# A streaming encoder step: row blocks of the up-projection loaded by GpSimd, and the row projection's operands placed alike within 512 bytes

## Chip, cores and metric

The kernel runs on one core of a Trainium2 chip, as one launch. The metric is the device time of that launch in microseconds (us). The comparison is between medians of runs; the profile is of one execution.

## What is computed

One inference step of an encoder trunk of depth 1, for 2048 prompt rows and 64 sample rows with the same weights, all float32. Cut to what the change touches:

```python
x = layer_norm(x, ln_in_g, ln_in_b)                       # 2112 rows x 1024
q, k, v, z, xbc, dt_raw, u, vc = split_cols(x @ w_in, IN_SIZES)
...                                                       # attention, SSD scan, gated MLP, RMS norms
x = layer_norm(DN_ALPHA * x + mixed @ w_out, ln1_g, ln1_b)
up, ffn_conv_state = causal_dwconv(x @ ffn_w_in, ffn_conv_prev, ffn_conv_w, ffn_conv_b)
gate, val = split_cols(up, (D_FF, D_FF))                  # D_FF = 2816
x = layer_norm(DN_ALPHA * x + (jax.nn.silu(gate) * val) @ ffn_w_out, ln2_g, ln2_b)
```

## The kernel before

Seven stages follow one another: row projection, feature projection, attention, SSD and gated MLP, output projection, up-projection (`ffn_up`), down-projection. Every float32 product is three matmuls on rounded parts: high x high, high x low, low x high (`products`, lines 129 to 131; lines 3037 to 3039 in the up-projection). For that each operand is split: a cast to the high part on ScalarE, a subtraction for the low part on VectorE.

**Row projection** (`project_rows`, tensor names `pr_`). The columns of `w_in` that are wanted by rows (v, z, the two gated-MLP parts and dt: 1286) are loaded in eight k blocks of 128 rows into `w_raw`, and split into `w_hi` and `w_lo`, both [128, 8, 1286]. Seventeen row tiles of 128 rows follow. A tile is normalised, turned by eight transposes into `ps_t` (line 449), copied and split into `xt_hi` and `xt_lo`, and is then the stationary operand of 72 matmuls into `ps_y`: 24 each against columns 0 to 511, 512 to 1023 and 1024 to 1285. In tile 0 k is the outer loop, since the weights are still arriving; in the others the column group is.

Where these operands start in a partition, by the built program, modulo 512 bytes:

| operand | before | after |
|---|---|---|
| `w_hi`, 512-wide columns | 256 + 24 k | 256 |
| `w_lo`, 512-wide columns | 448 + 24 k | 256 |
| high part, last 262 columns | 256 + 24 k | 256 + 24 k |
| low part, last 262 columns | 448 + 24 k | 448 + 24 k |
| `xt_hi`, `xt_lo` (each k block 512 bytes long) | 128 | 256 |

In the output projection, which runs the same 128x128 by 512 matmuls (`mo_ps_y`), weights and rows all start at 384.

**Up-projection** (`ffn_up`, names `fu_`). The rows are taken in three passes (q = 0, 1, 2) of 704 rows, each as two halves of 352, and the product of a 2 x 2 block matrix is formed with seven products in place of eight (Winograd's form). A unit is one step j of 22 in a pass: it takes 128 columns of the gate half and 128 of the value half of `ffn_w_in`, and has 7 products x 4 k blocks x 3 = 84 matmuls of 354 (in the last pass 356) columns. `mm_done` counts products, seven a unit.

The pass's rows lie in `xb`, seven slots of [4 k blocks x 356]. Four of them are loaded from `x1t`, the turned rows of the stage before (`X_B11`, `X_B21`, `X_T1`, `X_B22`, 708 KB each), and the others are differences that VectorE makes in units 20 and 21 of the pass before (`differences`). Once all seven slots are split into `x_hi` and `x_lo` (`x_lo_done` at 7 for each pass), `xb` may be loaded again. Pass 0's blocks are loaded in the output projection. Those of pass q + 1 are loaded by `load_x` on SyncE at the end of unit 1 of pass q. Its order there is written out by hand in `body`: per unit the raw weights for unit j + 2 (`load_raw`, line 2452), the stores of the previous unit's results (`store_h`: `h_mix` from `val1`, line 2501, `h_val` from `val0`, line 2506; `store_sums`), the store of the split weights to `fu_w_split` in pass 0 and their load in passes 1 and 2 (lines 2553 and 2559), and in pass 1 loads and stores of `load_late` and `store_late`. SyncE issues all of these in that order, each after its wait.

ScalarE writes `val0` again for the next unit (`tap0_c21`) once `h_stored[0]` says that the last store of it has landed, and `val1` likewise with `h_stored[1]`. Behind that instruction on ScalarE stands the copy of TensorE's first product of the unit (`p1`, line 2728), without which TensorE's third product does not start.

In `ffn_up` GpSimd does only two small memsets (lines 2655 and 2656), once `x_lo_done` is at 14.

Of the kernel before, what the change touches and what calls it, by code (L numbers as in the profile page):

```python
# [26 lines left out]
P = 128  # L27
# [124 lines left out]
def project_rows(nc, d):  # L152
# [8 lines left out]
    with nc.cleanup_on_exit(), ExitStack() as ctx:  # L161
# [15 lines left out]
        w_hi, w_lo = m.sb("w_hi", [P, KD, NW], F32R), m.sb("w_lo", [P, KD, NW], F32R)  # L177
        x = m.sb("x", [P, 2, D])
        xr = m.sb("xr", [P, 2, D])
        xt_hi, xt_lo = m.sb("xt_hi", [P, 2, KD, P], F32R), m.sb("xt_lo", [P, 2, KD, P], F32R)  # L180
# [45 lines left out]
        with nc.Block() as block:  # L226
# [87 lines left out]
            def _(act):  # L314
                def weights_hi(ks):
                    for k in ks:
                        act.wait_ge(w_loaded[k], 64)
                        act.copy(w_hi[:, k, :], w_raw[:, k, :]).then_inc(w_hi_done, 1)
# [48 lines left out]
            def _(dve):  # L367
                def weights_lo(ks):
                    for k in ks:
                        dve.wait_ge(w_hi_done, k + 1)  # L370
                        dve.tensor_tensor(w_lo[:, k, :], w_raw[:, k, :], w_hi[:, k, :].bitcast(F32),
                                          ALU.subtract).then_inc(w_lo_done, 1)
# [68 lines left out]
            def _(pe):  # L441
# [12 lines left out]
                def step(t, p, i):  # L454
# [10 lines left out]
                    def product(k, x):  # L465
                        out, a, w = x
                        return products(pe, out, xt_hi[:, p, k, :n], xt_lo[:, p, k, :n],
                                        w_hi[:, k, a:a + w], w_lo[:, k, a:a + w], k == 0, k == KD - 1)
# [1802 lines left out]
def ffn_up(nc, d):  # L2271
# [12 lines left out]
    with nc.cleanup_on_exit(), ExitStack() as ctx:  # L2284
# [71 lines left out]
            "xb_zeroed", "rest_loaded", "xb_loaded", "t_done", "x_hi_done", "x_lo_done", "s_done", "w_hi_done", "w_lo_done"))  # L2356
        raw_loaded = [m.sem("raw_loaded0"), m.sem("raw_loaded1")]
# [86 lines left out]
        with nc.Block() as block:  # L2444
            @block.sync
            def _(sp):
# [10 lines left out]

                def x_block(slot, ks, g, q, done):
                    r = PW * q + 352 * g
                    if q == NQ - 1:  # L2460
                        sp.dma_start(xb[:, slot, :, 0:GAP], d["x1t"][:, ks, r - H:r + LASTP]).then_inc(done, 16)
                        if g:
                            sp.dma_start(xb[:, slot, :, SMP:], d["x1t"][:, ks, SEQ:ROWS]).then_inc(done, 16)
                        else:
                            sp.dma_start(xb[:, slot, :, GAP:], d["x1t"][:, ks, r + LASTP - H:r + 352]).then_inc(done, 16)
                    elif r == 0:
                        sp.dma_start(xb[:, slot, :, H:H + 352], d["x1t"][:, ks, 0:352]).then_inc(done, 16)
                    else:
                        sp.dma_start(xb[:, slot, :, 0:H + width(q)], d["x1t"][:, ks, r - H:r + width(q)]).then_inc(done, 16)

                def load_x(q):
                    lo_k, hi_k = slice(0, KH), slice(KH, KD)
                    x_block(X_B11, lo_k, 0, q, xb_loaded[0])
                    x_block(X_B21, hi_k, 0, q, xb_loaded[1])
                    x_block(X_T1, lo_k, 1, q, rest_loaded)
                    x_block(X_B22, hi_k, 1, q, rest_loaded)
# [88 lines left out]
                def body(q, j, p):  # L2565
# [37 lines left out]
                    if isinstance(j, int) and j == 1 and q + 1 < NQ:  # L2603
                        sp.wait_ge(x_lo_done, 7 * (q + 1))
                        load_x(q + 1)
# [10 lines left out]
            def loaded_x(q):  # L2616

                return (16 * (q + 1), 32 * (q + 1)) if q < NQ - 1 else (16 * q + 32, 32 * q + 64)

            def differences(eng, q):  # L2620
# [5 lines left out]
                def t3_step():  # L2626
                    eng.wait_ge(xb_loaded[0], loaded_x(q)[0])
                    eng.wait_ge(xb_loaded[1], loaded_x(q)[0])
                    eng.wait_ge(rest_loaded, loaded_x(q)[1])
                    eng.wait_ge(xb_zeroed, 2 if q == NQ - 1 else 1)  # L2630
                    if q == NQ - 1:
                        eng.wait_ge(late_stored, 16 * LATE)
                    if q:
                        eng.wait_ge(x_lo_done, 7 * q)
                    eng.tensor_tensor(t3, b22, b12, ALU.subtract).then_inc(t_done, 1)
# [16 lines left out]
            @block.gpsimd  # L2652
            def _(pool):
                pool.wait_ge(x_lo_done, 7 * (NQ - 1))
                pool.memset(xb[:, X_T1, :, GAP:SMP], 0.0)
                pool.memset(xb[:, X_B22, :, GAP:SMP], 0.0).then_inc(xb_zeroed, 1)

            @block.scalar
            def _(act):
# [16 lines left out]
                def split_x_hi(q, slot):  # L2676
                    n = H + width(q)
                    if slot < 2:
                        act.wait_ge(xb_loaded[slot], loaded_x(q)[0])
                        act.wait_ge(xb_zeroed, 1)  # L2680
                    else:
                        act.wait_ge(t_done, 4 * q + {X_T2: 3, X_T1: 2, X_T3: 1, X_B22: 1, X_T4: 4}[slot])
                    if q:
                        act.wait_ge(mm_done, 7 * (KF * q - 1) + slot + 1)
                    act.copy(x_hi[:, slot, :, :n], xb[:, slot, :, :n]).then_inc(x_hi_done, 1)
# [880 lines left out]
```

## Time and profile before

| | us |
|---|---|
| median of three runs | 2599.79 |
| lowest and highest of them | 2592.39, 2600.45 |
| profiled execution | 2602.54 |
| its span, first to last instruction | 2601.0 |

| part of the span | from, us | to, us |
|---|---|---|
| row projection, TensorE | 12.8 | 281.9 |
| output projection, 48 matmuls of one tile | 1000.79 | 1011.78 |
| up-projection, pass 0, units 0 to 21 | 1185.5 | 1516.6 |
| pass 1 | 1516.6 | 1836.0 |
| pass 2 | 1836.0 | 2143.9 |

The engines are PE (TensorE; PEld is its loading of the stationary operand), DVE (VectorE), ACT (ScalarE), POOL (GpSimd) and SP (SyncE); SPq and POOLq are their instruction queues, which issue DMAs. A row of the timeline is the start, the duration, the instruction, and in brackets how long its engine had been idle before it and who ended that. A duration on TensorE overlaps the next, so matmuls are compared by their starts. Idle time costs something only on an engine that is waited for. [...]

### The profile page before, as it was taken

Reading aid. Unit: us, or ns where it says so; the run is one execution under the profiler, and the core shown is the slowest. Engines: PE = TensorE matmul, PEld = TensorE weight load, DVE = VectorE, ACT = ScalarE, POOL = GpSimd, SP = SyncE. Lnnn points to the kernel's source line nnn. Section 1 sums busy time; section 2 is a strip of 40 time slices with the busy share of each in tenths; the row PEclk is TensorE's granted clock in tenths of the full one; section 3 lists DMA queues with packets and bytes.
Section 4 is the critical chain, followed back from the end, with each engine's and each line's share of the span. In section 5 each row is a group of like instructions: output and inputs, shape, how many; then the busy total and the mean of one; then the engine's idle time right before and its main releaser. Section 6 shows DMA issues by size and latency. Waiting matters only on the chain. (4 is left out here: it accounts for less than half of the span.)

```text
span 2601.0 us, 45346 instructions
## 1 busy us (share of the span) xinstructions
PE 2489.1 (96%) x14723; PEld 2301.3 (88%) x14723; DVE 1798.1 (69%) x3398; ACT 1117.2 (43%) x2109; POOL 199.4 (8%) x271
## 2 busy tenths in 40 slices
PE   6999999998999989998999999999999999999998
PEld 5888899998999978887999989999899998888787
DVE  5434375556776777787899987777877775455787
ACT  4445322225665542325555554444545453322231
POOL 0001100020002850110000000000000000000000
PEclk9999999998998989999999999999999999999999
DMA  6446565556544654647777789998787867575564
GB/s 209 146 143 213 178 212 189 194 176 161 134 126 136 196 173 157 210 155 247 256 243 248 233 281 335 300 309 281 262 262 251 263 201 209 141 221 144 163 172 140
DMA packets 466762, 537.65 MB, mean 207 GB/s; under 512 B 68170, under 2 KB 388204, under 8 KB 465218
## 3 DMA queue, kind: packets, MB, share of 16 engines
q1 hardware_dynamic: 442204, 452.25, 55.9%
q0 software_dynamic: 19408, 62.38, 7.4%
q10 hardware_dynamic: 5030, 21.46, 2.4%
q8 instruction: 71, 1.16, 0.2%
q14 instruction: 49, 0.40, 0.0%
HBM read 349.87 MB, written 189.00 MB: 207 GB/s over the span
## 5 line engine op out<-in xcount | busy, mean ns | idle before, releaser
L3037 PE MATMUL fu_banks<-mo_fu_x_hi,mo_fu_w 128*128 128x354 f32 (+1 forms) x1848 | 608.4, 329 | 37.7 <-DVE fu_c L2994 12.8
L3039 PE MATMUL fu_banks<-mo_fu_x_hi,mo_fu_w 128*128 128x354 f32 (+1 forms) x1848 | 603.8, 327 | 0.0
L3038 PE MATMUL fu_banks<-fu_x_lo_rest,mo_fu_w 128*128 128x354 f32 (+1 forms) x1584 | 517.5, 327 | 0.0
L3037 PEld LDWEIGHTS fu_banks<-mo_fu_x_hi,mo_fu_w 128*128 128x128 f32 x1848 | 351.4, 190 | 51.6 <-DVE mo_fu_w L2850 11.7
L3039 PEld LDWEIGHTS fu_banks<-mo_fu_x_hi,mo_fu_w 128*128 128x128 f32 x1848 | 351.7, 190 | 0.0
L3038 PEld LDWEIGHTS fu_banks<-fu_x_lo_rest,mo_fu_w 128*128 128x128 f32 x1584 | 301.4, 190 | 0.0
L3302 ACT CAST fu_fd_h_hi<-fu_fd_h_raw 128x768 fp32r<-128x768 f32 (+1 forms) x116 | 88.1, 760 | 255.4 <-DMA fu_fd_h_raw<-fd_h_sum 104.3
L3347 DVE TENSOR_TENSOR fu_fd_h_a<-fu_fd_h_raw,fu_fd_h_hi 128x768 fp32r<-128x768 f32 x108 | 95.6, 889 | 147.1 <-ACT fu_fd_h_hi L3302 147.0
L129 PE MATMUL pr_ps_y<-pr_w_hi,pr_xt_hi 128*128 128x512 f32 (+3 forms) x408 | 148.3, 364 | 5.0 <-DVE pr_xt_lo L406 5.0
L130 PE MATMUL pr_ps_y<-pr_w_lo,pr_xt_hi 128*128 128x512 f32 (+3 forms) x408 | 147.5, 362 | 0.0
L131 PE MATMUL pr_ps_y<-pr_w_hi,pr_xt_lo 128*128 128x512 f32 (+3 forms) x408 | 146.8, 360 | 0.0
L2691 ACT ACTIVATE fu_gate<-fu_c,fu_vecs 128x352 f32<-128x352 f32 (+1 forms) x132 | 90.1, 682 | 74.8 <-DVE fu_c L2974 67.9
L2868 DVE SCALAR_TENSOR_TENSOR fu_gate<-fu_c,fu_vecs,fu_gate 128x352 f32<-128x352 f32 (+1 forms) x132 | 76.9, 583 | 58.9 <-ACT fu_gate L2691 58.9
L1432 PE MATMUL at_ps_o<-pf_at_v,at_pt 128*128 (+2 forms) x900 | 111.7, 269 | 0.0
L129 PE MATMUL mo_ps_y<-sg_mo_w_hi,sg_mo_mt_hi 128*128 128x512 f32 (+1 forms) x272 | 108.2, 398 | 2.7 <-PEq L1481 2.7
L1432 PEld LDWEIGHTS at_ps_o<-pf_at_v,at_pt 128*128 128x128 f32 (+1 forms) x900 | 107.9, 191 | 1.1
L130 PE MATMUL mo_ps_y<-sg_mo_w_lo,sg_mo_mt_hi 128*128 128x512 f32 (+1 forms) x272 | 106.6, 392 | 0.0
L131 PE MATMUL mo_ps_y<-sg_mo_w_hi,sg_mo_mt_lo 128*128 128x512 f32 (+1 forms) x272 | 106.6, 392 | 0.0
L129 PE MATMUL fu_banks<-fu_fd_wa,fu_fd_h_hi 128*128 128x512 f32 x256 | 100.2, 392 | 4.3 <-DVE fu_fd_h_a L3347 3.4
L2845 DVE TENSOR_TENSOR mo_fu_w<-fu_w_raw,mo_fu_w 128x1024 fp32r<-128x1024 f32 x65 | 79.5, 1223 | 29.4 <-ACT mo_fu_w L2664 29.4
L130 PE MATMUL fu_banks<-fu_fd_wa,fu_fd_h_hi 128*128 128x512 f32 x256 | 99.7, 389 | 0.0
L131 PE MATMUL fu_banks<-fu_fd_wa,fu_fd_h_a 128*128 128x512 f32 x256 | 99.6, 389 | 0.0
(458 smaller groups left out, 5987.0 us busy)
## 6 DMA issues: line engine op xcount, KB each, us to landing
mo_fu_w<-fu_w_split SPq DMA_DIRECT2D x176, 512.0 KB, 5.0
fu_w_split<-mo_fu_w SPq DMA_DIRECT2D x44, 1024.0 KB, 5.8
fu_w_raw<-ffn_w_in SPq DMA_DIRECT2D x87, 512.0 KB, 5.4
fd_w_sum<-pf_fdw_sum ACTq DMA_DIRECT2D x11, 1024.0 KB, 5.0
fu_w_raw<-ffn_w_in SPq DMA_DIRECT2D x44, 256.0 KB, 6.0
pf_fdw_raw<-ffn_w_out ACTq DMA_DIRECT2D x9, 1024.0 KB, 8.0
x_rows<-pr_xr SPq DMA_DIRECT2D x16, 512.0 KB, 2.9
xt<-pr_xt SPq DMA_DIRECT2D x16, 512.0 KB, 4.0
```

The source lines that it names most:

```text
L129: pe.matmul(out, lhs_hi, rhs_hi, start=first, stop=False)
L130: pe.matmul(out, lhs_hi, rhs_lo, start=False, stop=False)
L131: return pe.matmul(out, lhs_lo, rhs_hi, start=False, stop=last)
L1432: last = pe.matmul(ps_o[:b.nq, par, 0:HD], pt[:w, par, k, :b.nq], vals, start=(k == 0), stop=(k == b.nb - 1))
L2691: act.activation(out, src[:, 0:n], ACT.Identity, bias=one(vecs[:, 3, :], mt), scale=one(vecs[:, 0, :], mt)).then_inc(tap0_done, 1)
L2845: dve.tensor_tensor(w_lo[:, p, W_A11:W_A12 + 1], w_raw[:, p, 0].rearrange("p (a k) c -> p a k c", a=2), w_hi[:, p, W_A11:W_A12 + 1].bitcas ...
L2868: dve.scalar_tensor_tensor(out=out, in0=src[:, 1:1 + n], scalar=one(vecs[:, 1, :], mt), in1=out, op0=ALU.mult, op1=ALU.add).then_inc(tap1_ ...
L3037: pe.matmul(out, wh, xh, start=first and k == 0, stop=False, skip_group_check=True)
L3038: pe.matmul(out, wh, xl, start=False, stop=False, skip_group_check=True)
L3039: last = pe.matmul(out, wl, xh, start=False, stop=k == KH - 1, skip_group_check=True)
L3302: act.copy(h_hi[:, n % RING, 0:raw.shape[1], 0:raw.shape[2]], raw).then_inc(h_hi_done, 1)
L3347: dve.tensor_tensor(low, raw, high.bitcast(F32), ALU.subtract).then_inc(h_lo_done, 1)
```

## The change

The first part splits the row projection's weights: the first 1024 columns keep the names `w_hi` and `w_lo`, now [128, 8, 1024], and the last 262 get tensors of their own, `w_hi_b` and `w_lo_b`. A tensor of 128 bytes that nobody uses, `beside`, stands before `xt_hi`. The table above has the places that come of it. Each of the eight casts and eight subtractions of the weights is now two instructions. The feature projection's operands keep their places.

The second part takes `load_x` from SyncE. GpSimd issues the same DMAs: for pass q, after `x_lo_done` at 7 q, the four blocks one at a time, block n after `mm_done` at 7 (22 (q - 1) + 3 n + 5), that is when unit 3 n + 4 of the pass before is done: at the starts of units 5, 8, 11 and 14. One semaphore, `x_loaded`, counts them, and both ScalarE and VectorE wait for all of a pass's. For pass 2 GpSimd does its memsets first.

```diff
-        w_hi, w_lo = m.sb("w_hi", [P, KD, NW], F32R), m.sb("w_lo", [P, KD, NW], F32R)
+
+        NA = 1024
+        w_hi, w_lo = m.sb("w_hi", [P, KD, NA], F32R), m.sb("w_lo", [P, KD, NA], F32R)
+        w_hi_b, w_lo_b = m.sb("w_hi_b", [P, KD, NW - NA], F32R), m.sb("w_lo_b", [P, KD, NW - NA], F32R)
         x = m.sb("x", [P, 2, D])
         xr = m.sb("xr", [P, 2, D])
+        beside = m.sb("beside", [P, 32])
...
-                        act.copy(w_hi[:, k, :], w_raw[:, k, :]).then_inc(w_hi_done, 1)
+                        act.copy(w_hi[:, k, :], w_raw[:, k, 0:NA])
+                        act.copy(w_hi_b[:, k, :], w_raw[:, k, NA:]).then_inc(w_hi_done, 1)
...
-                        dve.tensor_tensor(w_lo[:, k, :], w_raw[:, k, :], w_hi[:, k, :].bitcast(F32),
+                        dve.tensor_tensor(w_lo[:, k, :], w_raw[:, k, 0:NA], w_hi[:, k, :].bitcast(F32), ALU.subtract)
+                        dve.tensor_tensor(w_lo_b[:, k, :], w_raw[:, k, NA:], w_hi_b[:, k, :].bitcast(F32),
                                           ALU.subtract).then_inc(w_lo_done, 1)
...
-                        return products(pe, out, xt_hi[:, p, k, :n], xt_lo[:, p, k, :n],
-                                        w_hi[:, k, a:a + w], w_lo[:, k, a:a + w], k == 0, k == KD - 1)
+                        high, low = (w_hi[:, k, a:a + w], w_lo[:, k, a:a + w]) if a < NA else (w_hi_b[:, k], w_lo_b[:, k])
+                        return products(pe, out, xt_hi[:, p, k, :n], xt_lo[:, p, k, :n], high, low, k == 0, k == KD - 1)
...
-                    if isinstance(j, int) and j == 1 and q + 1 < NQ:
-                        sp.wait_ge(x_lo_done, 7 * (q + 1))
-                        load_x(q + 1)
...
             def _(pool):
-                pool.wait_ge(x_lo_done, 7 * (NQ - 1))
-                pool.memset(xb[:, X_T1, :, GAP:SMP], 0.0)
-                pool.memset(xb[:, X_B22, :, GAP:SMP], 0.0).then_inc(xb_zeroed, 1)
+                def x_block(slot, ks, g, q):
+                    r = PW * q + 352 * g
+                    if q == NQ - 1:
+                        pool.dma_start(xb[:, slot, :, 0:GAP], d["x1t"][:, ks, r - H:r + LASTP]).then_inc(x_loaded, 16)
+                        if g:
+                            pool.dma_start(xb[:, slot, :, SMP:], d["x1t"][:, ks, SEQ:ROWS]).then_inc(x_loaded, 16)
+                        else:
+                            pool.dma_start(xb[:, slot, :, GAP:], d["x1t"][:, ks, r + LASTP - H:r + 352]).then_inc(x_loaded, 16)
+                    else:
+                        pool.dma_start(xb[:, slot, :, 0:H + width(q)], d["x1t"][:, ks, r - H:r + width(q)]).then_inc(x_loaded, 16)
+
+                lo_k, hi_k = slice(0, KH), slice(KH, KD)
+                for q in range(1, NQ):
+
+                    pool.wait_ge(x_lo_done, 7 * q)
+                    if q == NQ - 1:
+                        pool.memset(xb[:, X_T1, :, GAP:SMP], 0.0)
+                        pool.memset(xb[:, X_B22, :, GAP:SMP], 0.0).then_inc(xb_zeroed, 1)
+                    for n, (slot, ks, g) in enumerate(((X_B11, lo_k, 0), (X_B21, hi_k, 0), (X_T1, lo_k, 1), (X_B22, hi_k, 1))):
+
+                        pool.wait_ge(mm_done, 7 * (KF * (q - 1) + 3 * n + 5))
+                        x_block(slot, ks, g, q)
```

SyncE in pass 0, from unit 0's last issues over unit 1 to the loop that begins with unit 2, before (`mo_fu_xb` is `xb`, `fu_val` is `val0` or `val1`):

```order
L2452 DMA fu_w_raw<-ffn_w_in 128x8x128 x2
L2501 DMA fd_h_mix<-fu_val 128x352
L2506 DMA fd_h_val<-fu_val 128x352
L2553 DMA fu_w_split<-mo_fu_w 128x2x1024 x2
L2469 DMA mo_fu_xb<-x1t 128x4x354 x4
L2387 UNCONDITIONAL_BRANCH
```

and after:

```order
L2459 DMA fu_w_raw<-ffn_w_in 128x8x128 x2
L2488 DMA fd_h_mix<-fu_val 128x352
L2493 DMA fd_h_val<-fu_val 128x352
L2540 DMA fu_w_split<-mo_fu_w 128x2x1024 x2
L2394 UNCONDITIONAL_BRANCH
```

The four loads are gone from the end of unit 1, and the raw weights for unit 4 (the loop's first DMA) follow the weight stores. At the same place of pass 1 eight loads are gone in the same way.

GpSimd in the up-projection, before:

```order
L2652 UNCONDITIONAL_BRANCH
L2655 MEMSET mo_fu_xb 128x4x2
L2656 MEMSET mo_fu_xb 128x4x2
L2444 UNCONDITIONAL_BRANCH
```

and after:

```order
L2640 UNCONDITIONAL_BRANCH
L2651 DMA mo_fu_xb<-x1t 128x4x354 x4
L2658 MEMSET mo_fu_xb 128x4x2
L2659 MEMSET mo_fu_xb 128x4x2
L2645 DMA mo_fu_xb<-x1t 128x4x290
L2649 DMA mo_fu_xb<-x1t 128x4x66
```

Twelve DMAs now stand on GpSimd's queue, four with 354 columns in pass 0, and in pass 1 eight: four of 290 columns, two of 66 and two of 64.

## Rows read from the trace of the kernel before

**Rows 1.** The page's busy time, share of the span and instructions of each engine.

```profile
PE 2489.1 (96%) x14723; PEld 2301.3 (88%) x14723; DVE 1798.1 (69%) x3398; ACT 1117.2 (43%) x2109; POOL 199.4 (8%) x271
```

**Rows 2.** Waits of TensorE, whole span: engine, tile, line, releaser: us in total, times, longest.

```profile
PE fu_banks L3037 <- DVE fu_c L2994: 12.8, 26, 1.6
PE fu_banks L3037 <- ACT fu_part L2728: 9.0, 4, 3.7
```

**Rows 3.** Timeline of TensorE: start, us, line, operands; row projection, then output projection.

```profile
163.73 0.48 PE L129 MATMUL pr_ps_y<-pr_w_hi,pr_xt_hi 128*128 128x512 f32 x1
...
174.96 0.28 PE L129 MATMUL pr_ps_y<-pr_w_hi,pr_xt_hi 128*128 128x262 f32 x1
...
1000.79 0.48 PE L129 MATMUL mo_ps_y<-sg_mo_w_hi,sg_mo_mt_hi 128*128 128x512 f32 x1
...
1011.78 0.49 PE L2237 MATMUL mo_ps_t<-ident,mo_y 128*128 128x128 f32 x3
```

**Rows 4.** Waits of ScalarE in the up-projection's passes 0 and 1 (1206 to 1836 us).

```profile
ACT fu_val L2691 <- DMA fd_h_val<-fu_val: 7.1, 1, 7.1
ACT fu_val L2691 <- DMA fd_h_mix<-fu_val: 5.9, 1, 5.9
```

**Rows 5.** SyncE queue timeline: end of unit 1, passes 0 and 1; last row unit 6.

```profile
1220.67 5.34 SPq L2469 DMA_DIRECT2D mo_fu_xb<-x1t  x4
...
1231.83 2.92 SPq L2501 DMA_DIRECT2D fd_h_mix<-fu_val  x1
...
1549.21 1.31 SPq L2461 DMA_DIRECT2D mo_fu_xb<-x1t  x1
...
1557.26 1.32 SPq L2463 DMA_DIRECT2D mo_fu_xb<-x1t  x1
...
1564.60 0.43 SPq L2506 DMA_DIRECT2D fd_h_val<-fu_val  x1
...
1616.02 0.37 SPq L2506 DMA_DIRECT2D fd_h_val<-fu_val  x1
```

**Rows 6.** Units 3, 9 (pass 0), 3, 9, 8 (pass 1): us, busy, clock, DMA, GB/s.

```profile
1235.49:1254.77 19.28, 15.98 (x87) 15.12 (x85) 13.79 (x22) 9.61 (x16) 0.00 (x0) 0.91 0.76 260
1326.27:1340.42 14.15, 13.92 (x85) 13.64 (x85) 13.21 (x21) 8.17 (x14) 0.00 (x0) 1.00 0.77 248
1562.88:1581.99 19.11, 15.45 (x86) 15.16 (x85) 10.87 (x21) 6.10 (x11) 0.00 (x0) 0.91 1.08 363
1650.80:1664.73 13.93, 13.93 (x86) 13.64 (x85) 10.54 (x21) 6.30 (x11) 0.00 (x0) 1.00 0.89 282
1637.15:1650.80 13.65, 13.65 (x86) 13.65 (x85) 10.21 (x20) 6.41 (x11) 0.00 (x0) 1.00 1.06 341
```

**Rows 7.** Groups of ScalarE's casts by width, and TensorE's first product of the row projection.

```profile
L318 ACT CAST pr_w_hi<-pr_w_raw 128x1286 fp32r<-128x1286 f32 x8 | 9.9, 1263 | 6.7 <-DMA pr_w_raw<-w_in 6.6
...
L2664 ACT CAST mo_fu_w<-fu_w_raw 128x1024 fp32r<-128x1024 f32 x20 | 20.7, 1036 | 0.0
...
19.77 0.80 PE L129 MATMUL pr_ps_y<-pr_w_hi,pr_xt_hi 128*128 128x512 f32 x1 [4.99 <-DVE pr_xt_lo L406]
```

**Rows 8.** Windows: pass 1 from unit 6 to 19, and 3 us of pass 0.

```profile
1609.50:1802.00 192.50, 192.50 (x1175) 190.50 (x1174) 144.90 (x266) 88.40 (x155) 0.00 (x0) 1.00 0.97 308
1321.00:1324.00 3.00, 2.74 (x17) 2.45 (x15) 2.65 (x4) 2.77 (x5) 0.00 (x0) 1.00 0.13 46
```

**Rows 9.** Stores of fu_val (pass 1), and timeline of ScalarE in unit 3 and unit 7.

```profile
DMA to landing us min/median/max: 1.9/4.6/5.3
...
1569.57 0.64 ACT L2691 ACTIVATE fu_val<-fu_banks,fu_vecs 128x352 f32<-128x352 f32 x1 [7.07 <-DMA fd_h_val<-fu_val]
...
1623.52 0.65 ACT L2691 ACTIVATE fu_val<-fu_banks,fu_vecs 128x352 f32<-128x352 f32 x1 [0.71 <-PE fu_banks L3039]
```

**Rows 10.** Timeline of VectorE and of GpSimd's queue in the row projection.

```profile
173.75 1.28 DVE L400 SCALAR_TENSOR_TENSOR pr_xr<-pr_xr,pr_rs,pr_b_bc 128x1024 f32<-128x1024 f32 x1
...
174.42 0.53 POOL L267 DMA_DIRECT2D pr_x<-x_prompt  x1 [15.70 <-DVE pr_xr L397]
```

More of the change, by code:

```diff
@@ L2356, in ffn_up @@
             "xb_zeroed", "rest_loaded", "xb_loaded", "t_done", "x_hi_done", "x_lo_done", "s_done", "w_hi_done", "w_lo_done"))
+        x_loaded = m.sem("x_loaded")
         raw_loaded = [m.sem("raw_loaded0"), m.sem("raw_loaded1")]
@@ L2456, in load_raw @@
                         load_half(j, p, half, raw_loaded[p], q)
[L2458 to L2476, printed above, removed]
                 load_half(0, 0, 1, raw_loaded[0])
@@ L2614, in _, with x_there @@
                     sp.wait_ge(w_stored[p], 32 * (KF // 2))
-            def loaded_x(q):
-                return (16 * (q + 1), 32 * (q + 1)) if q < NQ - 1 else (16 * q + 32, 32 * q + 64)
+            def x_there(eng, q, slot=None):
+                if q:
+                    eng.wait_ge(x_loaded, 16 * (4 if q < NQ - 1 else 12))
+                    return
+                for s in range(2) if slot is None else (slot,):
+                    eng.wait_ge(xb_loaded[s], 16)
+                if slot is None:
+                    eng.wait_ge(rest_loaded, 32)
             def differences(eng, q):
@@ L2626, in t3_step @@
                 def t3_step():
-                    eng.wait_ge(xb_loaded[0], loaded_x(q)[0])
-                    eng.wait_ge(xb_loaded[1], loaded_x(q)[0])
-                    eng.wait_ge(rest_loaded, loaded_x(q)[1])
+                    x_there(eng, q)
                     eng.wait_ge(xb_zeroed, 2 if q == NQ - 1 else 1)
@@ L2678, in split_x_hi @@
                     if slot < 2:
-                        act.wait_ge(xb_loaded[slot], loaded_x(q)[0])
+                        x_there(act, q, slot)
                         act.wait_ge(xb_zeroed, 1)
```

## The prediction

> **What bounds the kernel now.** First the busy shares: TensorE is busy 96% of the span [rows 1], so only two things can shorten the kernel: less time per matmul, or fewer of the gaps in which TensorE has nothing to do. TensorE's waits in the up-projection are mostly for VectorE's `fu_c`, 12.8 us in 26, and for ScalarE's `fu_part`, 9.0 us in only 4 [rows 2]: many small ones and a few large. Second, the timeline of TensorE: the row projection and the output projection run the same matmul, 128x128 against 512 columns. Durations overlap, so I go by starts. In the row projection the 48 matmuls of 512 columns of one row tile go from 163.73 to 174.96 us, 11.23 us, 234 ns each; in the output projection 48 go from 1000.79 to 1011.78, 10.99 us, 229 ns each [rows 3]. [...] Third, the waits of ScalarE in the up-projection: over the first two passes it waits for a transfer twice only, once 7.1 us (for the store of `fu_val` to `fd_h_val`) and once 5.9 us (the store to `fd_h_mix`) [rows 4]. Fourth, SyncE's queue at these two places: the four loads of `mo_fu_xb` take 5.34 us to issue from 1220.67 on in the first pass; the eight of the second begin at 1549.21 and the last ends at 1558.58. The stores that ScalarE waited for stand behind them: 1231.83 (2.92 us to issue one) and 1564.60 [rows 5]. Last, the windows by unit. A unit is 84 matmuls. Unit 3 takes 19.28 us in pass 0 and 19.11 in pass 1, at a granted clock of 0.91, where another odd unit takes 14.15 and 13.93 at 1.00 [rows 6].
>
> **Part 1, the row projection's places.** What it changes is where operands start within 512 bytes. Before, `w_hi` starts at 256 and `w_lo` at 448, each of the eight k blocks 24 bytes further on, the rows (`xt_hi`, `xt_lo`) at 128. After, all the 512-wide operands and the rows start at 256. The output projection has all of its at 384: the state that part 1 makes, and there 48 matmuls take 10.99 us. So the term is 11.23 - 10.99 = 0.24 us a tile, times 17 tiles = 4.1 us. Nothing else in that stage ends late: the row of tile starts is bound by TensorE throughout, and the stage's end moves with its last matmul. That the start is the reason is inferred: the shapes are the same, the clock is full, neither stretch has a wait. So the lower bound is 0. The 262-wide matmuls (`w_hi_b`, `w_lo_b`) keep their steps of 24 bytes and move only against the rows; I give them 0, with bounds of the same 5 ns each way: 17 x 24 = 408 matmuls x 5 ns = 2.0 us.
>
> What it adds: eight casts on ScalarE and eight subtractions on VectorE, since each k block is split in two instructions. A cast of 1286 columns is 1263 ns and one of 1024 is 1036 [rows 7], so 0.87 ns a column, and the 262-wide one would be 228 ns if it had no fixed part; the fixed part (1036 less 1024 x 0.87) is some 150 ns. TensorE's first product waits for `pr_xt_lo` [rows 7], and that stands behind three casts of which the first two wait for their loads, so one fixed part lies on the path: 0.15 us. The other splits run while TensorE works on tile 0. Bounds 0 and 8 x 0.15 = 1.2 us. Net of part 1: 4.1 - 0.15 = 3.9 us.
>
> [...]
>
> **Part 2, the row blocks.** Removed: four (pass 0) and eight (pass 1) DMAs from SyncE's queue at the end of unit 1. They cost nothing as transfers, they cost as a queue: the issue takes SyncE 5.34 us in pass 0 and 9.37 us in pass 1, and the store of unit 2 behind them goes out at 1564.60, 15.4 us after unit 2 began (13.65 us, the length of an even unit, before unit 3's 1562.88 [rows 6], so 1549.2), where in unit 6, begun at 1609.5, the same store goes out at 1616.02, 6.5 us in [rows 5]. That is 8.9 us late, about the 9.37 us of issue. Price by the windows: 19.28 - 14.15 = 5.1 us and 19.11 - 13.93 = 5.2 us, together 10.3 us; the half clock that follows each gap is in it. What is late next in unit 3: by the odd units without a burst nothing but the short wait for VectorE that each of them has, and that is in the 14.15.
>
> Added: the same 708 KB four times a pass, on GpSimd's queue, at the starts of units 5, 8, 11 and 14. GpSimd has nothing else to do in this stage; the wait for `mm_done` keeps up nobody. The data are needed at unit 20, six units of 14 us after the last load, so the landing is hidden. What isn't hidden by itself is the bandwidth. 725,000 bytes at the 363 GB/s of the busiest unit [rows 6] are 2.0 us. In pass 0 each unit has a hole: DMA share 0.13 over 3 us [rows 8], 2.6 us free, cost 0. In pass 1 the share is 0.97 at 308 GB/s [rows 8], so the block pushes what SyncE has in flight back by up to 2.0 us. Nearest to biting is the store of `fu_val`: issued 1616.02, landing in at most 5.3 us, so by 1621.3, and ScalarE comes to the buffer at 1623.52 [rows 5, 9]: 2.2 us of slack, before TensorE's own. 2.0 is under 2.2; cost 0. Upper bound: all 2.0 us four times, 8.0 us. Even in the burst itself the store issued at 1564.60 had landed 5.0 us later, when ScalarE went on at 1569.57 [rows 9]; it was the issue that was late, not the transfer. I therefore stay at 0.
>
> GpSimd issuing beside a busy VectorE: the one at 174.42 (0.53 us) falls within the VectorE instruction of 173.75, which takes its usual 1.28 us [rows 10]. Cost 0; the bound is 12 issues x 0.53 = 6.4 us if each held VectorE up, of which pass 0's four, 2.1 us, would count, since there TensorE waits for VectorE in every unit.
>
> [...] [Rows 10] show an issue of 0.53 us beside VectorE.
>
> **Sum.** 3.9 + 10.3 = 14.2 us. The profiled execution took 2602.5 us (span 2601.0), so it would be 2588.3. The median of the three runs, 2599.8, is 2.7 below it; I forecast against the median: 2585.6 us.
>
> **The rivals.**
> [...]
> - The new loads stall pass 1. For: share 0.97. Against: the 5.0 us landing in the burst. 14.2 - 8.0 = 6.2 us gained: 2593.6 us.
> - The stall of unit 3 stays, because the transfers and not SyncE's issue made it, or another transfer has the same lateness. Only part 1 is left: 2599.8 - 3.9 = 2595.9 us.
> - Slower: each of the eight GpSimd loads brings a stall like today's. Place: the store of `fu_val` in the unit of the load; price: 5.2 us each with its half clock, 8 x 5.2 = 41.6 less 14.2, +27.4: 2627.2 us. It decides when the store lands over 7.5 us after its issue (5.3 + 2.2); in the present burst it was 5.0.
>
> **How the numbers follow.** Forecast case 0.70; no effect of places 0.10; stalls in pass 1 0.11; unit 3 keeps its stall 0.05; slower 0.04. A measurement of this kernel can tell about 0.3%, 7.8 us. Faster by more than that is nearly all of the forecast case, two thirds of the second and a few of the third: 0.77. Within: 0.19. Slower: 0.04. The range goes from 2578 (the forecast less 2.0 for the 262-wide matmuls and 5 for the spread of runs, which is 2592.4 to 2600.5 before) to 2596 (the third and fourth case). Outside it is the slower case and the tails.
>
> **What would show it.** Part 1: 48 matmuls of 512 columns in 10.99 us per tile; the first product no more than 0.2 us later than 19.77. If it stays 11.23, the place is not the reason. Part 2: no wait of ScalarE for a transfer in the first two passes; unit 3 of both at 14.2 and 13.9 us and at full clock; units 5, 8, 11 and 14 as long as their neighbours. A wait for `fd_h_val` or `fd_h_mix` in units 8 or 14 of pass 1 would be the second rival; VectorE instructions longer than before beside GpSimd's issues, the price I put at 0. My prediction is wrong in its core if unit 3 keeps 19 us.

## The result and the profile after

The changed kernel takes 2585.4 us, median of 21 runs (2579.0 to 2595.1), the kernel before 2599.3, median of 21 (2592.4 to 2608.8). The medians are 13.9 us apart. The ratio is 0.9941, with a 95% interval of 0.9931 to 0.9951, which is 15.3 us less (13 to 18); 14.2 were forecast. The profiled execution took 2594.0 us (span 2592.5). That is 8.6 us above its kernel's median, so it shows the places, and the runs show the size.

Busy time of the engines, from the page of the changed kernel (against [rows 1]):

```profile
PE 2481.5 (96%) x14723; PEld 2296.8 (89%) x14723; DVE 1799.0 (69%) x3406; ACT 1118.5 (43%) x2117; POOL 208.1 (8%) x283
```

TensorE is busy 7.6 us less with the same 14723 instructions. VectorE, ScalarE and GpSimd have the eight or twelve instructions more that the change gives them.

**The row projection.** Timeline of TensorE in the changed kernel, the first matmul of 512 columns of one row tile and the first of 262 (against [rows 3]; start, us, line, operands):

```profile
162.12 0.48 PE L129 MATMUL pr_ps_y<-pr_w_hi,pr_xt_hi 128*128 128x512 f32 x1
...
173.12 0.28 PE L129 MATMUL pr_ps_y<-pr_w_hi_b,pr_xt_hi 128*128 128x262 f32 x1
```

The 48 matmuls take 11.00 us, where they took 11.23 (a row of 0.48 us and a next start some 0.23 us on: they overlap in both). It is the same in tiles 2 to 14, all at the full clock (11.00 or 11.01, before 11.23 or 11.24); the last two tiles take 11.04, before 11.25 and, for the last with its 64 rows, 11.12. The first interval of a tile is some 318 ns in both kernels. The next few are 227 to 236 ns and all later ones 226.7, in all three kinds of product; before they were 227 to 241 ns. After the first, the mean is 227.2 ns, before 232.2.

The start of this stage (against [rows 7]): the timeline of TensorE, and then the groups of ScalarE's casts by width, with busy time and mean ns after the bar, then the idle time before them and who ended it:

```profile
13.47 1.94 PE L455 MATMUL pr_ps_t<-ident,pr_xr 128*128 128x128 f32 x8 [13.47 <-DVE pr_xr L406]
20.41 0.80 PE L129 MATMUL pr_ps_y<-pr_w_hi,pr_xt_hi 128*128 128x512 f32 x1 [5.00 <-DVE pr_xt_lo L412]
```

```profile
L322 ACT CAST pr_w_hi<-pr_w_raw 128x1024 fp32r<-128x1024 f32 x8 | 8.3, 1044 | 6.9 <-DMA pr_w_raw<-w_in 6.9
...
L323 ACT CAST pr_w_hi_b<-pr_w_raw 128x262 fp32r<-128x262 f32 x8 | 3.2, 405 | 0.0
```

The pair of casts takes 1.45 us where one took 1.26. The wait before the first product is 5.00 us, before 4.99. All of this stage begins 0.6 us later, but so does TensorE's first instruction, which no part of the change touches: in the fourteen traces of this document it starts at 12.8 to 14.7 us, with and without the first part.

**The up-projection.** Windows of units 3 of passes 0 and 1, of unit 6 of pass 0, and of unit 8 of pass 1 (against [rows 6]; us, then busy time of PE, PEld, DVE, ACT and POOL, granted clock, DMA share, GB/s; the granted clock is TensorE's share of its full clock, the DMA share the mean busy share of the 16 DMA engines):

```profile
1236.12:1250.28 14.16, 13.93 (x86) 13.64 (x85) 13.21 (x21) 8.19 (x14) 0.00 (x0) 1.00 0.77 249
1558.86:1572.79 13.93, 13.92 (x86) 13.64 (x85) 10.57 (x21) 6.30 (x11) 0.00 (x0) 1.00 0.91 290
1278.83:1293.52 14.69, 14.13 (x85) 13.60 (x85) 13.41 (x22) 8.53 (x14) 0.00 (x0) 1.00 0.73 239
1627.96:1641.60 13.64, 13.64 (x85) 13.64 (x85) 10.21 (x20) 6.40 (x11) 1.49 (x2) 1.00 1.01 324
```

Unit 3 has lost its hole in both passes: 19.28 to 14.16 us and 19.11 to 13.93, 10.3 us together, at the full clock where the granted clock was 0.91. Unit 8 of pass 1, in which GpSimd issues a block, is as long as it was. Unit 6 of pass 0 is 0.3 us longer (14.69, before 14.40), and so is unit 15 (14.40, before 14.14).

Waits of ScalarE for transfers in passes 0 and 1 (against [rows 4]; us in total, times, longest), and SyncE's queue where the two late stores stood (against [rows 5]):

```profile
ACT fu_val L2698 <- DMA fd_h_mix<-fu_val: 2.8, 3, 1.1
ACT fu_val L2698 <- DMA fd_h_val<-fu_val: 1.0, 1, 1.0
```

```profile
1229.24 0.38 SPq L2488 DMA_DIRECT2D fd_h_mix<-fu_val  x1
...
1552.01 0.37 SPq L2493 DMA_DIRECT2D fd_h_val<-fu_val  x1
```

13.0 us in two waits have become 3.8 us in four. The store of pass 1 goes out 6.8 us after unit 2 began (1545.2), near the 6.5 of unit 6 [rows 5], and no longer 15.4.

GpSimd's first issue in its timeline, and then its line of pass 0 in the view by line (ns at least, median and most; first and last start):

```profile
1265.48 0.78 POOL L2651 DMA_DIRECT2D mo_fu_xb<-x1t  x1 [92.97 <-PE fu_banks L3046]
```

```profile
L2651 POOL DMA_DIRECT2D mo_fu_xb<-x1t x4: 751/756/782, 1265.5 to 1393.8; - x4
```

An issue takes 0.75 to 0.78 us and lands 5.9 to 8.9 us later. VectorE's busy time is 1799.0 us, before 1798.1.

**Where the time went**, in the two profiled executions, stage by stage from first matmul to first matmul: TensorE's start +0.6 us, row projection -3.5, feature projection +1.7, attention -2.3, SSD +3.8, output projection +0.3, from the up-projection to the end -9.0. The middle ones are no effect of the change: no instruction of these stages differs, and three traces of the changed kernel have 131.4, 120.7 and 117.0 us for the SSD stage. The two stages that were changed give 12.5 us. The 9.0 of the second is less than the 10.3 of the two units 3. Units 6 and 15 took 0.5 back, and the last two units of pass 1 are 0.7 longer (34.0 us together, before 33.3); in the other traces of versions without a burst these two vary from 33.2 to 34.2, so I don't put that down to the change.

### The profile page after: what moved, and what is told of

Its sections match the earlier page's. It is cut to its first block and busy times, and to the rows that moved or that the text cites. A ratio compares the mean times of both kernels' runs of the same rounds, so it can differ in the third digit from the quotient of the medians.

```text
span 2592.5 us, 45361 instructions
## 1 busy us (share of the span) xinstructions
PE 2481.5 (96%) x14723; PEld 2296.8 (89%) x14723; DVE 1799.0 (69%) x3406; ACT 1118.5 (43%) x2117; POOL 208.1 (8%) x283
## 5 line engine op out<-in xcount | busy, mean ns | idle before, releaser
L129 PE MATMUL pr_ps_y<-pr_w_hi,pr_xt_hi 128*128 128x512 f32 (+1 forms) x272 | 108.6, 399 | 5.0 <-DVE pr_xt_lo L412 5.0
L130 PE MATMUL pr_ps_y<-pr_w_lo,pr_xt_hi 128*128 128x512 f32 (+1 forms) x272 | 106.9, 393 | 0.0
L131 PE MATMUL pr_ps_y<-pr_w_hi,pr_xt_lo 128*128 128x512 f32 (+1 forms) x272 | 106.8, 393 | 0.0
```

The costliest lines, as they stand in the source:

```text
L129: pe.matmul(out, lhs_hi, rhs_hi, start=first, stop=False)
L130: pe.matmul(out, lhs_hi, rhs_lo, start=False, stop=False)
L131: return pe.matmul(out, lhs_lo, rhs_hi, start=False, stop=last)
```

## The experiments

Twelve more runs were made, of ten kernels: the changed kernel twice more, one version twice, and eight others. Ratios are to the kernel before, on the same chip and in the same rounds.

### One part at a time

The kernel before with the first part of the change alone (its diff stands above, the second part left away):

> The first part alone (the row projection's weights split and its rows moved by 128 bytes); the row blocks stay on SyncE. My account: 48 matmuls of 512 columns in 10.98 us a tile as in the changed kernel's trace, row projection 3.6 to 4.1 us shorter, unit 3 of passes 0 and 1 still 19.1 to 19.3 us; ratio to before 0.9985 (3.9 us). Rival, the two parts share a cause (the clock or the run): the tiles are shorter and the median is not, ratio 1.000.

Timeline of TensorE, the same two matmuls as above, and the windows of units 3:

```profile
162.94 0.48 PE L129 MATMUL pr_ps_y<-pr_w_hi,pr_xt_hi 128*128 128x512 f32 x1
...
173.94 0.28 PE L129 MATMUL pr_ps_y<-pr_w_hi_b,pr_xt_hi 128*128 128x262 f32 x1
```

```profile
1238.42:1258.09 19.67, 15.97 (x86) 15.11 (x85) 13.79 (x22) 9.61 (x16) 0.00 (x0) 0.91 0.75 255
1566.16:1587.75 21.59, 15.61 (x86) 15.32 (x85) 10.75 (x21) 6.08 (x11) 0.00 (x0) 0.84 1.02 332
```

The ratio is 0.9991 (0.9974 to 1.0007), 2596.0 against 2600.1 us. The tile has its 11.00 us, but the runs can't tell the kernel from no change: 2.3 us less, between 6.8 less and 1.8 more. The forecast's 3.9 lies inside. In this trace the holes of unit 3 were 2.9 us larger (19.67 and 21.59 us) than in the trace of before. That is one execution of each, so I can't say that a row projection that ends earlier always pays some of it back there.

The changed kernel with the first part undone:

> The second part alone (row blocks by GpSimd, one in three units); the row projection as before. My account: tiles of 11.23 us as before, unit 3 at 14.2 and 13.9 us, gain 10.3 us, ratio 0.9960. If both parts are independent, the two ratios multiply to the 0.9941 of the whole change. Rival, gains that overlap: this one alone already gives 13 us or more.

```profile
164.91 0.48 PE L129 MATMUL pr_ps_y<-pr_w_hi,pr_xt_hi 128*128 128x512 f32 x1
...
176.14 0.28 PE L129 MATMUL pr_ps_y<-pr_w_hi,pr_xt_hi 128*128 128x262 f32 x1
```

The same two matmuls are 11.23 us apart again, and the units 3 are 14.16 and 13.93 us. The ratio is 0.9963 (0.9949 to 0.9978), 9.6 us less. The two parts multiply to 0.9954, and the whole is 0.9941 (0.9931 to 0.9951), so they add up within their intervals.

The changed kernel itself, twice more beside other versions:

> The changed kernel once more, beside its two halves on one chip: ratio 0.994, and a second trace of it. The first trace's SSD stage was 3.8 us longer than that of the kernel before although no line of it changed; my account: that is the spread of executions, and here it is not longer by as much. Rival: the new row projection brings it, and it is again 3.8 us longer.

> The changed kernel once more, beside the version in which SyncE issues the single blocks. Ratio to the kernel before 0.992 to 0.995. Units 3 of passes 0 and 1 at 14.16 and 13.93 us, the 48 matmuls of 512 columns of a row tile at 226.6 ns each.

The ratios are 0.9924 (0.9902 to 0.9946) and 0.9947 (0.9929 to 0.9966), the units 3 14.15 and 13.93, then 14.16 and 13.92 us, the 48 matmuls of the tile at 162.26 us of the third trace 11.00. The spans are 2583.7 and 2581.0 us. The SSD stage is 120.7 and 117.0 us, so it isn't the new row projection that made it 3.8 us longer in the first trace. Unit 6 of pass 0 is again a little long (14.64 and 14.54 us, against 14.40 in its even neighbours) and so is unit 15 (14.35 and 14.45, against 14.15).

### Was it SyncE's issue, or the burst?

The prediction said that unit 3's hole came from SyncE's queue, blocked while it issued four or eight loads, and that the transfers were not to blame (an issue is what the engine does to start a DMA; the DMA lands when its data have arrived). The change moves the loads to another queue and also spreads them. This version only moves them: GpSimd issues all four blocks at the end of unit 1, where SyncE did.

```diff
-                        pool.wait_ge(mm_done, 7 * (KF * (q - 1) + 3 * n + 5))
+                        pool.wait_ge(mm_done, 7 * (KF * (q - 1) + 2))
```

> The changed kernel with one edit: GpSimd issues all four blocks of a pass in a row after unit 1, at the time at which SyncE issued them before. My account (SyncE's issue was late, not the transfers): no unit 3 of 19 us; ScalarE waits for a store of fu_val by at most 1 to 2 us once or twice; ratio to before 0.994 to 0.996. Rival (the burst of 2.8 MB itself delays the stores, spacing is what helps): unit 2 or 3 at 17 us or more in both passes, ratio 0.998.

Windows of its units 3, and below them ScalarE's timeline where it waited in each (start, us, then in brackets how long it was idle and for whom):

```profile
1232.31:1252.28 19.97, 15.71 (x85) 15.14 (x85) 14.44 (x24) 9.72 (x16) 0.00 (x0) 0.91 0.77 265
1559.69:1578.91 19.22, 15.46 (x86) 15.17 (x85) 10.78 (x21) 6.21 (x11) 0.00 (x0) 0.91 1.06 362
```

```profile
1235.91 0.68 ACT L2698 ACTIVATE fu_val<-fu_c,fu_vecs 128x352 f32<-128x352 f32 x1 [5.88 <-DMA fd_h_mix<-fu_val]
...
1566.47 0.64 ACT L2698 ACTIVATE fu_val<-fu_banks,fu_vecs 128x352 f32<-128x352 f32 x1 [7.09 <-DMA fd_h_val<-fu_val]
```

The holes are back, with the same two waits to 0.02 us (5.89 and 7.07 before), and the ratio is 0.9983 (0.9969 to 0.9997), which the first part alone can account for. So moving the loads off SyncE's queue gains next to nothing; the prediction's reason is wrong. GpSimd's queue, SyncE's queue (L2503 and L2504 load `fu_late_raw`) and, last, the row of SyncE's queue in the changed kernel for the same DMA in the same unit:

```profile
1218.74 3.02 POOL L2651 DMA_DIRECT2D mo_fu_xb<-x1t  x4 [50.06 <-PE fu_banks L3046]
```

```profile
1225.42 4.24 SPq L2488 DMA_DIRECT2D fd_h_mix<-fu_val  x1
...
1549.06 5.54 SPq L2503 DMA_DIRECT2D fu_late_raw<-fd_h_val  x1
1554.70 2.60 SPq L2504 DMA_DIRECT2D fu_late_raw<-fd_h_mix  x1
...
1558.68 0.37 SPq L2493 DMA_DIRECT2D fd_h_val<-fu_val  x1
```

```profile
1548.16 1.09 SPq L2503 DMA_DIRECT2D fu_late_raw<-fd_h_val  x1
```

Two things are to be seen. SyncE has none of the blocks on its queue, and still one DMA takes it 5.54 us to issue, where the same takes 1.09 without a burst: the long issues come with what is in flight, not with what stands on SyncE's own queue. And the store of pass 1 goes out 12.6 us after unit 2 began (1546.04), 2.8 us sooner than before the change (15.4 us, [rows 5]), yet ScalarE gets it at the same time, 20.4 us after unit 2's start in both (1566.47 less 1546.04; before, 1569.57 [rows 9] less 1549.2). In this version the store is late by two things: it goes out 12.6 us into the unit, where that of unit 6 goes out 6.5 us in [rows 5], and it then takes 7.7 us to land. The median of its line, 2.1 us, is no measure for that, since it mixes two kinds: most stores of that line land in some 2 us, but those of the even units of pass 1, to which this one belongs, in 4.4 to 5.1 from unit 4 on. In the kernel before the store of unit 2 landed in 5.0 us, which is ordinary ([rows 9]: up to 5.3), so there all of its lateness was in going out. In pass 0 it is the other way round: the store goes out on time here (7.5 us after unit 2 began, as in the changed kernel), but its issue takes 4.24 us and ScalarE has it 10.5 us after the issue began (1235.91 less 1225.42), where the later ones of pass 0 land in 1.9 to 2.1. The lateness shifts between issue and landing; what all the late ones have in common is the burst in flight.

### One block at a time, by SyncE

The other half of the question: GpSimd issues nothing, and SyncE issues each block at the end of another unit (5, 7, 11 and 13).

```diff
...
+                    at = (1, 3, 4, 6, 7, KF // 2 - 1) if q + 1 < NQ else (1, KF // 2 - 1)
+                    for n, (a, b) in enumerate(zip(at, at[1:])):
+                        with sp.Fori(a, b) as i:
+                            body(q, 2 * i, 0)
+                            body(q, 2 * i + 1, 1)
+                        if q + 1 < NQ and n < 4:
+                            x_block(*blocks[n], q + 1)
...
```

> The changed kernel with the blocks issued by SyncE again, but one at a time, at the ends of units 5, 7, 11 and 13. My account: spacing on the same queue is enough, since one block's issue is 1.3 us (2.6 us in pass 1); no unit of 19 us, ratio to before 0.994, at most 0.5 us in units 6, 8, 12 and 14 of pass 1. Rival (the queue of GpSimd is what helps): units 6, 8, 12 and 14 of pass 1 are each 1 us or more longer than their neighbours, ratio 0.996 to 0.998.

> The row blocks one at a time again, issued by SyncE at the ends of units 5, 7, 11 and 13, GpSimd doing only its two memsets. Beside the changed kernel on the same chip. If it matters nothing who issues a block as long as the blocks come singly: the two medians lie within 2 us of each other and both ratios to the kernel before within 0.992 to 0.995. If GpSimd's issue costs something beside a busy VectorE, this one is 2 to 6 us faster than the changed kernel.

All waits of ScalarE for a transfer in passes 0 and 1 (trace of the first of the two), and the windows of units 3 (trace of the second):

```profile
ACT fu_val L2705 <- DMA fd_h_mix<-fu_val: 0.5, 1, 0.5
```

```profile
1223.12:1237.28 14.16, 13.93 (x86) 13.64 (x86) 13.20 (x21) 8.18 (x14) 0.00 (x0) 1.00 0.78 249
1545.30:1559.23 13.93, 13.93 (x86) 13.64 (x85) 10.57 (x21) 6.30 (x11) 0.00 (x0) 1.00 0.94 287
```

The ratios are 0.9920 (0.9892 to 0.9948) and 0.9943 (0.9925 to 0.9961). In the second set the changed kernel ran beside it: 2585.15 us against 2585.65. GpSimd is not needed for the gain; spreading is all of it. In the second trace ScalarE waits for a transfer once, for 1.0 us in unit 15 of pass 1, and no unit is longer for it.

Units 6 and 15 of pass 0 aren't lengthened here (14.40 and 14.15 us). The two versions issue in different units, so this alone doesn't say that GpSimd causes it. The traces do say what goes with it. The store of `fd_h_mix` in unit 5 of the changed kernel, and ScalarE's wait for it:

```profile
1271.98 1.25 SPq L2488 DMA_DIRECT2D fd_h_mix<-fu_val  x1
```

```profile
1277.62 0.69 ACT L2698 ACTIVATE fu_val<-fu_c,fu_vecs 128x352 f32<-128x352 f32 x1 [1.06 <-DMA fd_h_mix<-fu_val]
```

The store landed 5.4 us after its issue began; the store of `fd_h_mix` in unit 5 of the kernel before (1276.46) landed after 1.9. In these traces the unit behind such a wait is longer only where the wait is over some 0.8 us: waits of 1.06 and 1.02 us in units 5 and 14 go with 0.3 us more in units 6 and 15, and one of 0.70 in unit 11 with nothing in unit 12. In the trace with the first part undone GpSimd issues the same blocks in the same units, the waits are 0.41, 0.39 and 0.82 us, and units 6, 12 and 15 take 14.40, 14.40 and 14.20. So it isn't GpSimd's issuing as such, but a store that meets a block in flight and lands late, on a small scale.

### How much may be in flight, and where

Two blocks at a time (1.45 MB), after units 4 and 10:

```diff
-                        pool.wait_ge(mm_done, 7 * (KF * (q - 1) + 3 * n + 5))
+                        pool.wait_ge(mm_done, 7 * (KF * (q - 1) + 6 * (n // 2) + 5))
```

> The changed kernel, but GpSimd issues the four row blocks in two pairs: two when unit 4 of the pass before is done, two when unit 10 is, so 1.45 MB in flight at once in place of 0.73 or 2.9. Theory S (what stalls is the amount that is in flight at once, and it is the transfers that hold the stores back, whichever queue carries them): a pair takes about 4 us of transfers at 350 GB/s where one block takes 2 and the burst 8. ScalarE had some 2.2 us of slack in an odd unit of pass 1 by the rows of before, so a pair may cost up to 2 us in unit 6 or 7 and 12 or 13 of pass 1 and nothing in pass 0, in all 0 to 4 us: a ratio to the kernel before of 0.993 to 0.996. Rival F (the hole is made by four blocks or more only when they meet the stores of unit 2, so pairs are free): no unit is longer than its neighbours and the ratio is that of the changed kernel, about 0.993.

Window of unit 6 of pass 0 and of unit 6 of pass 1, and the rows of SyncE and ScalarE for the store that was late in pass 0:

```profile
1274.93:1291.12 16.19, 14.18 (x86) 13.60 (x85) 13.79 (x22) 9.61 (x16) 0.00 (x0) 1.00 0.65 231
...
1599.64:1613.30 13.66, 13.66 (x87) 13.66 (x86) 10.23 (x20) 6.40 (x11) 0.00 (x0) 1.00 1.07 368
```

```profile
1268.08 1.06 SPq L2488 DMA_DIRECT2D fd_h_mix<-fu_val  x1
```

```profile
1275.24 0.68 ACT L2698 ACTIVATE fu_val<-fu_c,fu_vecs 128x352 f32<-128x352 f32 x1 [2.58 <-DMA fd_h_mix<-fu_val]
```

A pair costs 1.8 us in unit 6 and 1.9 in unit 12 of pass 0 (16.19 and 16.33 against 14.40), and nothing in pass 1. I had put it the other way round, because I went by the DMA share of a whole unit, 0.77 in pass 0 and 1.07 here in pass 1. What goes with it is the one store that falls into the burst: it went out 7.3 us into unit 5, as in any odd unit, its issue took 1.06 us (0.37 otherwise), and ScalarE had it 7.2 us after that began. In pass 1 units 5 and 11 send no `fd_h_mix`; their store of `fd_h_val` landed after 6.1 us, and nobody waited for it. The ratio is 0.9962 (0.9948 to 0.9975), some 4 us worse than the changed kernel beside it (0.9947), but the two intervals overlap, so the runs alone don't tell them apart.

All four blocks in one burst, but after unit 7:

```diff
-                        pool.wait_ge(mm_done, 7 * (KF * (q - 1) + 3 * n + 5))
+                        pool.wait_ge(mm_done, 7 * (KF * (q - 1) + 8))
```

> The changed kernel, but GpSimd issues all four row blocks in one burst when unit 7 of the pass before is done, in place of at the ends of units 4, 7, 10 and 13. Theory S (the burst itself makes the stall): the stall comes back at another place, in unit 9 or 10 of passes 0 and 1, at 19 to 20 us in place of 14.15 and 13.93, with a wait of ScalarE for the store of fu_val of 5 to 7 us, and unit 3 stays at 14.16 and 13.93. The ratio to the kernel before is then about 0.998. Rival P (the place after unit 1 is what is bad, since the stage's first units still have other transfers behind them): unit 9 and 10 are as their neighbours and the ratio is about 0.993.

Windows of units 9 of passes 0 and 1, and of unit 3 of pass 0:

```profile
1312.71:1332.16 19.45, 15.97 (x85) 15.10 (x85) 13.79 (x22) 9.61 (x16) 0.00 (x0) 0.91 0.76 258
1637.26:1657.23 19.97, 16.64 (x86) 16.34 (x85) 10.95 (x22) 6.08 (x11) 0.00 (x0) 0.83 1.07 357
1227.04:1241.20 14.16, 13.92 (x85) 13.63 (x85) 13.21 (x21) 8.19 (x14) 0.00 (x0) 1.00 0.77 249
```

The hole has moved with the burst, with its size, from unit 3 to unit 9, and the ratio is 0.9988 (0.9972 to 1.0003). So in these traces one block costs 0 to 0.3 us, two cost 0 to 1.9, and four cost 5 to 6 at either place and from either queue (7.7 once, in pass 1 of the version with the first part alone).

### Which place counts

Three versions move the operands of the row projection against each other. `beside` also moves every tensor that stands behind the rows. Each version ran once, so only the trace is read; one execution's time (2585.3, 2593.8 and 2585.9 us, in this order) can't show 4 us. The rows (`xt_hi`, `xt_lo`) at 128 and the 512-wide weights at 256, by leaving `beside` out:

```diff
-        beside = m.sb("beside", [P, 32])
```

> The changed kernel without the unused tensor beside: all 512-wide weights start at 256 within 512 bytes for every k, the rows at 128. Theory A (what counts is where the two operands start against one another): the start-to-start of 512-wide matmuls goes back to 230 to 235 ns, a tile's 48 to 11.2 us. Theory B (what cost was the weights' steps of 24 bytes, off every power of two): it stays at 226.7 ns and 10.98 us.

The rows at 0 and the weights at 256, half of 512 bytes apart:

```diff
-        beside = m.sb("beside", [P, 32])
+        beside = m.sb("beside", [P, 96])
```

> The same with beside of 384 bytes: weights at 256, rows at 0, half of 512 bytes apart. Theory A: 230 ns or more, and a number of its own that differs from that of 128 apart. Theory B: 226.7 ns.

And the rows at 256 with the weights as before the change, each k block 24 bytes on from the last (the edit is shown against the version with the first part undone):

```diff
         xr = m.sb("xr", [P, 2, D])
+        beside = m.sb("beside", [P, 32])
...
```

> The second part of the change, and of the first part only the unused tensor: the rows start at 256, the weights are in one piece of 1286 columns with steps of 24 bytes (256 + 24 k and 448 + 24 k). Theory A: the high weights of k = 0, which start where the rows do, run at 227 ns, and those of the other blocks and all low weights at 228 to 240, by their distance; a tile's 48 at 11.1 to 11.3 us. Theory B: 232 ns for all, k = 0 too.

The same two matmuls of one tile in each, in this order:

```profile
165.36 0.48 PE L129 MATMUL pr_ps_y<-pr_w_hi,pr_xt_hi 128*128 128x512 f32 x1
...
176.61 0.28 PE L129 MATMUL pr_ps_y<-pr_w_hi_b,pr_xt_hi 128*128 128x262 f32 x1
```

```profile
162.18 0.48 PE L129 MATMUL pr_ps_y<-pr_w_hi,pr_xt_hi 128*128 128x512 f32 x1
...
173.18 0.28 PE L129 MATMUL pr_ps_y<-pr_w_hi_b,pr_xt_hi 128*128 128x262 f32 x1
```

```profile
164.32 0.48 PE L129 MATMUL pr_ps_y<-pr_w_hi,pr_xt_hi 128*128 128x512 f32 x1
...
175.53 0.28 PE L129 MATMUL pr_ps_y<-pr_w_hi,pr_xt_hi 128*128 128x262 f32 x1
```

11.25, 11.00 and 11.21 us. The first refutes the idea that the 24-byte steps of the weights are to blame: they are gone there, and the tile is as slow as before. The second shows that equal within 512 bytes isn't needed: at 256 bytes apart the intervals are what they are in the changed kernel, to 2 ns, so what counts here is the place within 256 bytes, as far as these three distances tell, and my expectation of a number of its own was wrong. The third shows that moving the rows without the weights gains 0.02 us a tile, and that moving the later tensors alone is not what helps. Its k block 0 is at 256 with its high part, like the rows, and still has 231 to 232 ns to the next start where I had expected 227.

A single interval can't be put down to its own operands. With the rows at 128 all eight k blocks stand alike, and still the intervals go from 228 to 241 ns: the long one, 239 to 241, comes at every seventh matmul, whichever block and kind of product it is. Only the sum over a tile is a measure of the place. What in the chip makes it is open, and distances other than 0, 128 and 256 bytes weren't tried by themselves.

The whole stage agrees. From TensorE's first matmul of it to the first of the feature projection it takes 274.1 to 274.7 us in the four traces with a tile above 11.2 us (the kernel before, the first part undone, rows at 128, rows moved only), and 269.9 to 271.4 in the ten with 11.00 us.

## Why the prediction was right, and where its reasons were not

**The time.** 2585.6 us was forecast and 2585.4 measured, and the range held. Both terms of the sum are also right by themselves, to some 1 us. That the medians agree to 0.2 us is luck: the gain that the ratio gives, 15.3 us, is only known to lie between 13 and 18.

**Part 1, 4.1 us less 0.15.** The step that took the output projection's 10.99 us as the goal holds: the tile went from 11.23 to 11.00, 0.23 x 17 = 3.9 us. The stage is 3.5 us shorter; the last tile, of 64 rows, gained 0.08 and not 0.23. The 262-wide matmuls moved from 122.4 to 121.6 ns on average, 0.3 us for all 408, within the bound of 2.0. The fixed part of the casts is real (405 ns for 262 columns, where 378 was worked out) but the wait before the first product grew by 0.01 us, not 0.15. The reason, the place of one operand against the other, was called inferred, and is now shown by the versions with rows at 128 and at 0, which differ from the changed kernel by the size of an unused tensor alone. That the operands would have to start at multiples of 256 bytes is no way out: in the output projection both start at 384 (128 modulo 256), and the 48 matmuls take 10.99 us [rows 3]. "Within 512 bytes" was wrong: of the distances that ran, 0 and 256 bytes are as good as each other, and 128 is not. A gain of 0 from the places, to which the prediction gave 0.10, did not come: it was 0.23 us a tile. That the clock plays no part in the difference is in the trace of the kernel before, where the granted clock is 1.00 in both stretches (163.7 to 174.9 us and 1000.8 to 1011.7).

**Part 2, 10.3 us.** The price by the windows is right to 0.1 us: 5.12 and 5.18 us by unit 3, 9.6 by the runs of this part alone. The half clock that the prediction counted in is in the trace of the kernel before: behind the gaps the granted clock is 0.50 from 1243.0 to 1246.0 us and from 1570.6 to 1574.0, and the matmuls of 354 columns there start some 295 ns apart, where at 1.00 (1246.3 to 1249.0) it is 163. The step that failed is the reason: "They cost nothing as transfers, they cost as a queue". The prediction saw a store go out late behind long issues and took the work of issuing for the cause. That the store of pass 1 went out late and landed in an ordinary 5.0 us is right. But that doesn't clear the transfers: with the loads on GpSimd's queue one DMA of SyncE still takes 5.54 us to issue (1.09 in the changed kernel), the store still goes out 6.1 us late, and ScalarE has it at the same time. The queue was held up by what was in flight. The rival with 0.05, "the transfers and not SyncE's issue made it", had the mechanism right and its consequence wrong: it let unit 3 keep its hole, but the change spreads the blocks as well, and that takes the cause away. So the forecast came out right by luck: two edits stood in one, and the one that I thought was only a matter of deadlines did the work. Had the change kept the burst, the same reasoning would have given 2585.6 us, and the runs of that version say 2595.9, beside 2600.1 for the kernel before.

**The new loads at 0.** Right in pass 1: units 5, 8, 11 and 14 are as long as their neighbours, at 1.01 of DMA share. In pass 0, which I held to be safe because of its free stretches, units 6 and 15 grew by 0.3 us each; the pairs show the same order, pass 0 first. The sign "no wait of ScalarE for a transfer in the first two passes" didn't come: there were four, of 0.7 to 1.1 us, and TensorE lost 0.5 us by them. The slack of 2.2 us was worked out for the store of `fd_h_val` in pass 1, and in pass 0 it is the store of `fd_h_mix` that is waited for first; that row was not priced.

**GpSimd beside VectorE at 0.** Right: VectorE's busy time grew by 0.9 us with eight instructions more, which are in the row projection. GpSimd's issues take 0.75 to 0.78 us beside a VectorE that is busy 293.6 of 316 us in pass 0 (from 1200 us on) and 248.4 of 320 in pass 1. What ran beside the twelve issues were TENSOR_TENSOR and SCALAR_TENSOR_TENSOR instructions only, 0.58 to 0.69 us each, so the trace says nothing of VectorE's other instructions.

**The slower case.** A single block never brought a stall like today's: the longest wait in passes 0 and 1 was 1.1 us. The limit that this case named, a store of `fd_h_val` that lands over 7.5 us after its issue, wasn't reached: the longest landings of pass 1 were 6.3 us (unit 8, nobody waited for it) and 5.8 (unit 14). The second went out 8.4 us into the unit and not 6.5, so ScalarE waited 1.0 us for it, and TensorE not at all (unit 15 took 13.93 us). A limit on the landing alone leaves out that a block in flight can also delay the issue.

## What to carry over

When a small store is late behind a large load, don't ask only in whose queue the load stands; ask how many bytes are in flight when the store goes out, and issue the load in pieces with work between them. Moving it to another engine's queue was no cure by itself here (2595.9 us against 2600.1, and unit 3 still at 19.97 and 19.22 us), while spreading it on the old queue was one (2585.65 us against 2601.1, unit 3 at 14.16 and 13.93): to tell the two apart, move it without spreading it, and spread it without moving it. And where a matmul of one shape takes two times in two stages, as the 11.23 and 10.99 us for 48 here, compare where the two operands start.

## What the runs showed that was not expected

- Matmuls of 128x128 by 512 columns at the full clock start every 226.7 ns when weights and rows begin at the same place within 256 bytes (the rows 0 or 256 bytes from the weights' 256; 48 in 11.00 us), and every 232 ns on average when they are 128 bytes apart (11.25 us).
- With 2.9 MB of loads in flight from GpSimd's queue, single DMAs on SyncE's took up to 5.54 us to issue (1.09 in the same unit without the burst), and a store of 176 KB landed after 7.7 us (4.4 to 5.1 in the later even units). Why the issue is held, and not only the landing, the traces don't show.
- The DMA share of a unit didn't tell where a load would cost something: with two blocks at once unit 6 of pass 1 took 13.66 us at a DMA share of 1.07 (an even unit of pass 1 before: 13.65 [rows 6]), while units 6 and 12 of pass 0, whose neighbours without a block have 0.77, were longer by 1.8 and 1.9 us.
